# Prompt attention of a hybrid decoder layer on one core: query blocks outermost, several heads in one step for short blocks, half of the first output-projection tiles inside the last steps

## The reference, cut to what matters

```python
# q: 8 query heads of 64, in 2 kv groups (G) of 4 heads (R); 512 tokens
s = einsum('btgrd,blgd->btgrl', q, k_branch) * 64 ** -0.5
p = masked_softmax(s, k_pos <= q_pos)
o = einsum('btgrl,blgd->btgrd', p, v_branch)      # branch: selected, window
o_nsa = g0 * o_compressed + g1 * o_selected + g2 * o_window
# then
mix = concat([conv_y, o_nsa]) @ w_out             # 1024 -> 1024: the output projection
h = x + rms_norm(mix, g_post)
f = square(relu(rms_norm(h, g_pre2) @ w_up)) @ w_down
y = h + rms_norm(f, g_post2)
```

## Time and profile before

| what | value |
|---|---|
| runs of the kernel before | 785.29, 785.44, 789.34 us; median 785.44 us |
| the profiled execution | 784.3 us, its span 782.5 us |
| TensorE busy over the span | 749.1 us (96%) |
| VectorE, ScalarE, GpSimd busy | 472.0, 251.0, 316.0 us |
| chain that ended last, by engine | PE 86%, DVE 7%, ACT 3%, issue 2%, DMA 1% |
| prompt attention, 254.44 to 348.59 us | 94.15 us |
| one weight block, issue to landing | 4.8 us (median of 46) |
| loads of blocks 13 and 14 issued by the sync engine | from 250.83 us, 1.65 us for both |

### The profile page before, as it was taken

One profiled execution on the slowest core, in us unless ns is written; L12 is line 12 of the kernel. 1 busy time (PEld: TensorE's weight loads), 2 busy tenths in 40 slices (PEclk: granted clock), 3 DMA queues, 4 the chain that ended last, 5 costly groups with the idle time before them and its releaser, 6 DMA issues.

```text
span 782.5 us, 14992 instructions
## 1 busy us (share of the span) xinstructions
PE 749.1 (96%) x6243; PEld 696.1 (89%) x6243; DVE 472.0 (60%) x713; ACT 251.0 (32%) x457; POOL 316.0 (40%) x130
## 2 busy tenths in 40 slices
PE   8999999999998988989999999999999999999993
PEld 7999999987897555669999999999999999999993
DVE  5999978788767777752287334710025776732236
ACT  6412532233655677661443121300001112110021
POOL 1100000122301300002515577766865867876774
PEclk9999999999999999999999999999999999999997
DMA  9532421356625931001134121252122232133103
GB/s 357 186 109 89 149 84 34 118 182 219 222 90 163 254 60 54 2 1 54 55 109 161 55 107 60 102 214 92 69 107 80 84 107 103 59 108 107 54 1 109
DMA packets 25042, 85.51 MB, mean 109 GB/s; under 512 B 7216, under 2 KB 12896, under 8 KB 17760
## 3 DMA queue, kind: packets, MB, share of 16 engines
q1 hardware_dynamic: 17760, 62.13, 24.3%
q0 software_dynamic: 3456, 16.78, 6.3%
q10 hardware_dynamic: 3776, 5.89, 2.0%
HBM read 80.51 MB, written 8.47 MB: 114 GB/s over the span
## 4 chain that ended last, share of the span: by engine, by line
PE 86%; DVE 7%; ACT 3%; issue 2%; DMA 1%; SPq 0%; DVEq 0%; ACTq 0%
PE PA L1510 28%; PE PB L1510 28%; PE PB L1832 5%; DVE smx L1316 2%; PE PR L1930 2%; PE PR L1684 1%; PE PB L1521 1%; PE PA L1521 1%; PE PS L1705 1%; PE PB L1946 1%; DMA wraw<-wblk_dram 1%; PE PA L1669 1%; PE PR L1611 1%; PE PS L1954 1%; PE PS L1611 1%
## 5 line engine op out<-in xcount | busy, mean ns | idle before, releaser
L432 POOL TENSOR_TENSOR wH<-wraw,zero 128x2048 fp32r<-128x2048 f32 x29 | 105.3, 3631 | 110.6 <-PE PB L1510 87.1
L435 POOL TENSOR_TENSOR wL<-wraw,wH 128x2048 fp32r<-128x2048 f32 x29 | 139.5, 4811 | 2.3
L1412 DVE TENSOR_TENSOR hL<-h,hH 128x520 f32 (+1 forms) x32 | 64.6, 2022 | 47.1 <-ACT hH L876 47.1
L874 ACT ACTIVATE h<-rl 128x520 f32<-128x520 f32 x32 | 20.4, 638 | 209.3 <-DVE rl L1407 208.6
L992 DVE SCALAR_TENSOR_TENSOR yC<-uP,vec,yC 128x512 f32<-128x512 f32 (+1 forms) x135 | 84.3, 686 | 0.1
L1510 PE MATMUL PA<-hL,wH 128*128 128x260 f32 x240 | 67.7, 282 | 0.0
L1510 PE MATMUL PB<-hL,wH 128*128 128x260 f32 x240 | 67.7, 282 | 0.0
L1510 PE MATMUL PA<-hH,wL 128*128 128x260 f32 x240 | 67.7, 282 | 0.0
L1510 PE MATMUL PA<-hH,wH 128*128 128x260 f32 x240 | 67.7, 282 | 0.0
L1510 PE MATMUL PB<-hH,wH 128*128 128x260 f32 x240 | 67.7, 282 | 0.0
L1510 PE MATMUL PB<-hH,wL 128*128 128x260 f32 x240 | 67.7, 282 | 0.0
(11 more groups left out here) (517 smaller groups left out, 2311.1 us busy)
## 6 DMA issues: line engine op xcount, KB each, us to landing
wraw<-wblk_dram SPq DMA_DIRECT2D x46, 1024.0 KB, 4.8
xT<-x_fm_dram SPq DMA_DIRECT2D x4, 520.0 KB, 5.0
xT<-x_fm_dram SPq DMA_DIRECT2D x1, 2080.0 KB, 12.0
y_fm_dram<-xT SPq DMA_DIRECT2D x8, 260.0 KB
rkw<-cwk_dram SPq DMA_DIRECT2D x8, 256.0 KB, 2.7
s_win_dram<-cwk_dram ACTq DMA_DIRECT2D x1, 2044.0 KB
s_win_dram<-cwv_dram ACTq DMA_DIRECT2D x1, 2044.0 KB
p_rows_dram<-ktok ACTq DMA_DIRECT2D x4, 256.0 KB, 3.2
```

The source lines that it names most:

```text
L432: pool.tensor_tensor(wH[1 - s][:, :], wraw[s][:, :], zero[:, :].broadcast_to([P, BW]), ALU.add)\
L435: pool.tensor_tensor(wL[1 - s][:, :], wraw[s][:, :], wH[1 - s][:, :].bitcast(F32), ALU.subtract)\
L874: act.activation(h2[c % 2][:, :], rl[c % 2][:, :], ACT.Square).then_inc(s_h2, 1)
L1412: dve.tensor_tensor(lo, h2[c % 2][:, :], hi.bitcast(F32), ALU.subtract).then_inc(s_hl, 1)
```

## The change

The order of the prompt's attention is turned: the query block `i` is outermost, then the branch, then the heads. For block 0 (128 keys) all four heads, 128 keys each, form one step; for block 1 (256 keys) two heads form one step; for blocks 2 and 3 a step is one head as before. 32 steps become 22 (2, 4, 8 and 8). Every step now fills 1024, 768 or 1024 score columns over both groups. The exponentials, the scaling, masks, scores and transposes are issued for each head and group as before; maxima, sums, inverses, the copy of the transposes and the value products are issued once for all heads of the step. `PS[:, i % 2]` collects all four heads of one query block, `oH` and `oL` are written by query block, and the compressed branch enters by four matmuls of 128 columns for each block. The splits of weight blocks 13 and 14 move to steps 6 and 12 (ScalarE), 8 and 14 (VectorE), in the new count.

The first 260 columns of the output projection need query blocks 0 and 1, and the first four queries of block 2 (256 to 259). So the first half of tile 0 is issued inside the loop, in pass 23, between the transposes of step 20 and the values of step 19; the first half of tile 1 follows the loop, before the wait for the last block's split. The second halves come after it.

```diff
-PAIRS = [(r, br, i) for r in range(R) for br in range(2) for i in range(QT)]
-N_PAIRS = len(PAIRS)
-PER_R = 2 * QT
+HEADS = (((0, 1, 2, 3),), ((0, 1), (2, 3)), ((0,), (1,), (2,), (3,)), ((0,), (1,), (2,), (3,)))
+STEPS = [(rs, br, i) for i in range(QT) for br in range(2) for rs in HEADS[i]]
+N_STEPS = len(STEPS)
+PROBS = [sum(2 * len(rs) for rs, _, _ in STEPS[:n]) for n in range(N_STEPS + 1)]
+I_END = [sum(2 * len(HEADS[j]) for j in range(i + 1)) for i in range(QT)]
...
+            def out_hi(i):
+                act.wait_ge(s_pv, I_END[i])
+                act.activation(oH[:, :, i * P:(i + 1) * P], PS[:, i % 2, :].rearrange("p (r q) -> p r q", r=R),
+                               ACT.Copy).then_inc(s_oh, 1)
...
+                    act.activation(PTb[u % 2][:, :, 0:n], PR[:, :, 0:n], ACT.Copy).then_inc(s_ev, 1)
...
+                    for x in range(len(rs)):
+                        for g in range(G):
+                            c = PROBS[s] + g * len(rs) + x
+                            act.activation(Pb[s % 3][:, g, x * n:(x + 1) * n], PZ[s % 2][:, g, x * n:(x + 1) * n],
+                                           ACT.Exp, bias=smx[:, c:c + 1], accum_out=sms[:, c:c + 1]).then_inc(s_ex, 1)
...
-                if s in (8, 16):
-                    block_hi(13 if s == 8 else 14)
+                if s in (6, 12):
+                    block_hi(13 if s == 6 else 14)
+                for i in range(QT - 1):
+                    if s == I_END[i] + LAG + 2:
+                        out_hi(i)
+            out_hi(QT - 1)
...
+                    if len(rs) > 1:
+                        scores = PZ[s % 2][:, :, :].rearrange("p g (r n) -> p (g r) n", n=n)
+                    else:
+                        scores = PZ[s % 2][:, :, 0:n]
+                    dve.tensor_reduce(smx[:, PROBS[s]:PROBS[s + 1]], scores, AX.X, ALU.max, negate=True)\
+                        .then_inc(s_mx, 1)
...
+                    for x, r in enumerate(rs):
+                        for g in range(G):
+                            gc = 8 * (1 + br) + g * R + r
+                            c = PROBS[u] + g * len(rs) + x
+                            dve.tensor_scalar(Pb[u % 3][:, g, x * n:(x + 1) * n], Pb[u % 3][:, g, x * n:(x + 1) * n],
+                                              smr[:, c:c + 1], gtok[:, i, gc:gc + 1], ALU.mult, ALU.mult)\
+                                .then_inc(s_pn, 1)
...
-                if s in (10, 18):
-                    block_lo(13 if s == 10 else 14)
+                if s in (8, 14):
+                    block_lo(13 if s == 8 else 14)
...
+                    for g in range(G):
+                        for x in range(nr):
+                            for j in range(i + 1):
+                                mm = pe.transpose(PR[:, g, (j * nr + x) * P:(j * nr + x + 1) * P],
+                                                  Pb[u % 3][:, g, x * n + j * P:x * n + (j + 1) * P], ident[:, :])
                     mm.then_inc(s_T, 1)
...
+                if s == N_STEPS + 1:
+                    pe.wait_ge(s_cvl, CT)
+                    pe.wait_ge(s_ol, QT - 1)
+                    pe.wait_ge(s_split, SPLITS(B_OUT))
+                    pe.wait_ge(s_ex, PROBS[N_STEPS - 1])
+                    half_group(B_OUT % 2, 0, PA, actH, actL, 0)
...
+                    for x, r in enumerate(rs):
+                        for g in range(G):
+                            h = slice(g * HD, (g + 1) * HD)
+                            mm = pe.matmul(PZ[s % 2][:, g, x * n:(x + 1) * n], qT[h, r, i * P:(i + 1) * P],
+                                           kT[h, br, 0:n], start=False, stop=True, skip_group_check=True)
                     mm.then_inc(s_S, 1)
...
+                            mm = pe.matmul(PS[g * HD:(g + 1) * HD, i % 2, rs[0] * P:rs[0] * P + n],
+                                           vtok[:, br, j, g * HD:(g + 1) * HD], PTb[w % 2][:, g, j * n:(j + 1) * n],
                                            start=False, stop=(j == i), skip_group_check=True)
                     mm.then_inc(s_pv, 1)
...
-            pe.wait_ge(s_ol, R)
-            pe.wait_ge(s_ex, 2 * N_PAIRS)
-            for k in range(KT - 2):
+            pe.wait_ge(s_ex, PROBS[N_STEPS])
+            half_group(B_OUT % 2, 1, PB, actH, actL, 0)
+            pe.wait_ge(s_ol, QT)
+            half_group(B_OUT % 2, 0, PA, actH, actL, 1, s_grp)
+            half_group(B_OUT % 2, 1, PB, actH, actL, 1, s_grp)
+            for k in range(2, KT - 2):
```

More of the change, by code:

```diff
@@ L1326, in _ @@
                     dve.wait_ge(s_sm, 2 * u + 2)
[L1327 to L1332, removed]
+                    for x, r in enumerate(rs):
[5 more added lines that the diff above has]
+                                .then_inc(s_pn, 1)
+                if s == 4:
                     dve.wait_ge(s_dA, DA_OH)
@@ L1338, in _ @@
                                             oH[h, :, TP:T].bitcast(F32), ALU.subtract))
-                if s in (10, 18):
-                    block_lo(13 if s == 10 else 14)
[L1341 to L1348, removed]
+                if s in (8, 14):
+                    block_lo(13 if s == 8 else 14)
+                for i in range(QT - 1):
+                    if s == I_END[i] + LAG + 2:
+                        out_lo(i)
+            out_lo(QT - 1)
             dve.wait_ge(s_cst2, 32)
@@ L1513, in group, with half_group @@
                 mm.then_inc(s_grp, 1)
-            def half_group(s, c, pz, src_h, src_l, hf, done, k0=0, first=True):
+            def half_group(s, c, pz, src_h, src_l, hf, done=None, k0=0, first=True):
                 cols = slice(hf * HT, (hf + 1) * HT)
@@ L1902, in _ @@
             pe.wait_ge(s_initd, 2)
-            for s in range(N_PAIRS + LAG + 1):
+            for s in range(N_STEPS + LAG + 1):
                 u, w = s - LAG, s - LAG - 1
-                if s < N_PAIRS:
-                    r, br, i = PAIRS[s]
+                if s < N_STEPS:
+                    rs, br, i = STEPS[s]
+                    n = (i + 1) * P
                     if s >= 2:
-                        pe.wait_ge(s_ex, 2 * (s - 1))
+                        pe.wait_ge(s_ex, PROBS[s - 1])
                     for g in range(G):
-                        pe.matmul(PZ[s % 2][:, g, i * P:(i + 1) * P], identb[:, :], maskb[:, :], start=True, stop=False,
-                                  skip_group_check=True)
+                        for x in range(len(rs)):
+                            pe.matmul(PZ[s % 2][:, g, x * n + i * P:(x + 1) * n], identb[:, :], maskb[:, :],
+                                      start=(x == 0), stop=False, skip_group_check=True)
                 if s == 3:
@@ L1935, in _ @@
                         pe.wait_ge(s_dA, DA_OD)
-                    if r == 1:
+                    if i == 1:
                         pe.wait_ge(s_dV, DV_P + 4)
-                    if r >= 2:
-                        pe.wait_ge(s_ol, r - 1)
-                    pe.matmul(PS[:, r % 2, :], vcBD[:, r % 2, :], PcT[:, r // 2, :], start=True, stop=False,
-                              skip_group_check=True)
-                if s < N_PAIRS:
-                    r, br, i = PAIRS[s]
-                    for g in range(G):
-                        h = slice(g * HD, (g + 1) * HD)
-                        mm = pe.matmul(PZ[s % 2][:, g, 0:(i + 1) * P], qT[h, r, i * P:(i + 1) * P], kT[h, br, 0:(i + 1) * P],
-                                       start=False, stop=True, skip_group_check=True)
+                    if i >= 2:
+                        pe.wait_ge(s_ol, i - 1)
@@ new lines, in _ @@
+                    for r in range(R):
+                        pe.matmul(PS[:, i % 2, r * P:(r + 1) * P], vcBD[:, r % 2, :],
+                                  PcT[:, r // 2, i * P:(i + 1) * P], start=(r == 0), stop=False, skip_group_check=True)
+                if s < N_STEPS:
+                    rs, br, i = STEPS[s]
+                    n = (i + 1) * P
+                    for x, r in enumerate(rs):
[3 more added lines that the diff above has]
+                                           kT[h, br, 0:n], start=False, stop=True, skip_group_check=True)
```

70 lines of the change are left out of this document (31 added, 39 removed).

## The result

The changed kernel takes 777.92 us (median of 4 runs, 777.54 to 779.56), the kernel before on the same chip 786.32 us (median of 4, 785.29 to 789.34). The ratio is 0.9886 with a 95% interval of 0.9863 to 0.9909: 9.0 us or 1.1% faster, between 7.2 and 10.8. The forecast was 778.2 us. The profiled execution took 778.18 us with a span of 775.7, 6.8 us less than the 782.5 of before.

What follows compares the result with a forecast made beforehand. TensorE was taken to bound the prompt's attention, with 76.7 us of work in 94.15; 4.8 + 0.3 - 1.1 + 0 + 3.2 = 7.2 us less gave 778.2 us, with 773.5 to 782.0 as the range for 8 in 10.

Steps and rivals of the forecast that it cites:

- the stage: Prompt's attention: forecast from first scores to first projection matmul, 94.15 to 86.9 us; measured to the third projection tile.
- TensorE's work, 4.8 less: Attention steps of blocks 0 and 1: grouping heads cuts TensorE's work from 25.0 to 20.2 us.
- the ends: Score pairs in grouped steps: lower end nothing more (taken), upper end full lone-pair price, 2.0 us more.
- exposed loads: Rival on grouped score pairs: each pays a lone pair's price for its own weights, about 781 us; chance 0.13.
- The end, 3.2 less: From last scores to output projection: waiting falls from 4.2 to 1.0 us, half tiles alone worth 1.5.
- S+14.4: S is the end of step 21's scores; the half tile covering the last split ends 14.4 us later.
- The clock, 1.1 more: TensorE's half-clock loss in attention grows by 1.1 us, after a longer standstill before step 2's mask.
- the first dip: Clock drop in the filling, at 261 us: expected to grow from about 2 to 3 us.
- keep the second: Attention's second clock drop, at 312 to 315 us before: expected to stay, wherever it falls.
- a sign of being wrong: In the profile after, a clock dip over 5 us was listed as showing the forecast wrong.
- The filling and the rest, 0.3 less: Pipeline filling and short waits: 4.1 us of waiting plus 1.0 for block changes and `out_hi`, 5.1 for 5.4.
- The weight splits, 0: Splits of weight blocks 13 and 14 beside query blocks 2 and 3: TensorE's waits stay at 4.4 us.

Runs made afterwards that it cites:

- single_heads: Changed kernel with one head in every step (32 steps), query blocks outermost and half tiles moved; 785.0 us, ratio 0.9972 to the kernel before.
- order_only: Changed kernel with both halves of projection tiles 0 and 1 after the loop again, order and grouping kept; 781.1 us, ratio 0.9929 to the kernel before.
- keep_clock: Changed kernel with 44 and 22 idle matmuls before the masks of steps 2 and 3; 775.3 us, ratio 0.9854 to the kernel before.
- clock_and_sample: Changed kernel with sample_early's move plus 24 idle matmuls before step 3's mask and 8 before the first transposes; 776.2 us, ratio 0.9854.
- no_splits: Changed kernel with the splits of weight blocks 13 and 14 cut to one column each (stale weights); 773.0 us, ratio 0.9817.
- sample_early: Changed kernel with the sample group's 20 small matmuls in pass 2 before the mask's wait, not pass 3 after it; 775.4 us, ratio 0.9846.
- all_three: Changed kernel with the edits of clock_and_sample and quarters together; 770.8 us, ratio 0.9793 to the kernel before.
- quarters: Changed kernel with the splits of weight blocks 13 and 14 in quarters of 512 columns, one a step; 775.1 us, ratio 0.9846.

## Why the prediction was right, point by point

The forecast for the stage was 7.2 us less and 7.06 came. The terms were not all as good as their sum: the end brought 0.7 less than forecast and the clock cost 0.6 more, and the rest of the stage made up for both without having been forecast. That the sum came within 0.2 us is in part luck; that most of the gain is TensorE's work saved by the grouping is not.

- *TensorE's work, 4.8 less.* By the chain, a step of block 0 costs 0.45 + 0.88 + 1.12 + 1.01 = 3.46 us (forecast 3.51), one of block 1 0.33 + 0.88 + 1.06 + 1.01 = 3.28 (3.29), the compressed branch 0.89 for 0.86. That gives 25.0 - 20.0 - 0.1 = 4.9. single_heads, which takes back the grouping alone, loses 4.7, but with 1.7 us more of half clock in it and shorter waits in the filling (1.55 us, for 2.62 and 1.33), so that the two numbers are alike is no proof to the tenth. The choice between the ends was right: score pairs with weights of their own cost their columns and nearly nothing more. The forecast read the Trainium skill's rule on weight loads ("TensorE: Matmul & The Clock Gate", Part 3, The mechanism) as speaking for exposed loads, which would have shown as 1.3 to 1.7 us; in this trace they are not on the path. The reading was doubtful: by that rule a load overlaps matmuls of another row group, and the score products go to the two groups' 64 rows in turn, so that each load does have another row group than the product just before it.
- *The end, 3.2 less.* From the end of step 21's scores (332.67 us) to the second half of tile 0 (347.78) pass 15.11 us; without the two halves' usual 5.75 it is 9.36, with 7.7 of attention work and 1.7 of waiting, for 4.2 before: 2.5 less. (The forecast's 7.68 of work is 7.74 by its own rows.) The forecast put the end at S+14.4, it came at S+15.1. Its order of waits was right, that of step 20's transposes for the emptied `PR` included, but each came a little later: those transposes ended 0.3 us later than forecast, the last values 0.5 later, and the half tile that follows them took 3.08 us for 2.88. The part due to the half tiles was given as 1.5 us; order_only measures 1.8.
- *The clock, 1.1 more.* The step in it that failed is the size of the first dip, and with it "keep the second": there was one dip, not two, but of ten microseconds, twice the 5 us that the forecast itself had named as a sign of being wrong. By the windows it loses 3 x (0.31 + 0.50 + 0.50 + 0.40) = 5.1 us against 3.4 before, 1.7 more. That the longer standstill in the filling would cost clock was right in place and kind; keep_clock, which shortens it, and clock_and_sample, which removes it, speak for that.
- *The filling and the rest, 0.3 less.* The waits were forecast at 2.8 us before step 2's mask (2.62) and the first scaling's end at 263.9 (263.8). But the sample group's matmuls ran at half clock (4.6 us on the path for 2.5), so the values of step 1 ended at 279.7 us, where the forecast had 275.0 at full clock, or 278 with the 3 us of its dip. After that block 1 ran without a wait, as forecast (the forecast's 2.9 us for VectorE there is 3.0 with its own 1.22 for the maximum, still under TensorE's 3.3), and nothing was lost where the block size changes, where 1.0 us had been allowed. What is left once the other terms are taken off is 7.06 - 4.9 - 2.5 + 1.7 = 1.4 us less, for 0.3; this row was not measured by itself, so why it is larger stays open.
- *The weight splits, 0.* The waits are 0.94, 1.94, 1.01 and 0.51 us, 4.4 in all, as forecast, though not in the forecast's even pattern: VectorE's split of block 13 costs TensorE almost nothing, and the two of block 14, where the steps grow from 768 to 1024 columns, cost 3.5. no_splits prices them at 4.9.

The moved half tiles and splits made nothing later late: the third tile follows without a wait.

What stays open: the medians differ by more than the spans, 8.4 and 6.8 us. The profiled execution of before, 784.3 us, is under all of that kernel's other runs (784.5 to 790.5 us in two other sessions), so the spans may understate the gain. Its longer runs are those with the lower mean clock, 0.990 at 784.5 us and 0.981 at 790.2; where in the kernel their clock fell no profile shows. The forecast's own 7.2 lies at the edge of the measured 7.2 to 10.8.

## What to carry to other kernels

In a pipeline over several engines, grouping short steps into one pays by what it takes off the engine that sets the pace, and that can be added up from the chain of waits before building it; the maximum, the copy and the matmuls with shared columns then cost what their total size does. But the largest steps came to stand in the filling, where nothing hides them: put other work in the standstill, for the wait itself and for TensorE's clock after it. A side job that is longer than an engine's spare time in one step should be cut into pieces of that size, and work of the next stage that needs only early results can stand in the last steps, above all to cover the final split.

## What the runs showed of the hardware

- TensorE's clock falls to 1.2 GHz after standstills that are short: 2.62 and 1.33 us in the filling, or a single 1.94 us between dense steps (0.56 of full in 303 to 306 us of sample_early, 0.75 and 0.68 in clock_and_sample), but the same 1.94 us wait in the changed kernel, order_only and keep_clock was followed by windows at 1.00. With one profile of each, that can lie in the build or in the execution. The Trainium skill ("TensorE: Matmul & The Clock Gate", Why this matters for your kernels) warns that idle gaps between bursts bring the half clock; the traces agree that the clock falls behind gaps, though not behind every one.
- It can fall without a standstill: in keep_clock the gaps were filled up to 263.5 us, then came 20 matmuls of 8 and 64 columns, and the clock was 0.79 and 0.64 in the next windows. In clock_and_sample and all_three the same matmuls stood 6 us earlier in the stage and it stayed at 1.00. What tells the two apart was not tried.
- In four of the nine profiles of the changed kernel and its edits (single_heads, no_splits, quarters, clock_and_sample) the clock also fell in 249 to 255 us, ahead of everything that was edited, and the stage began 1.7 to 2.1 us later. Two windows of quarters:

```profile
249.00:252.00 3.00, 1.96 (x40) 1.91 (x41) 0.86 (x2) 0.79 (x2) 0.00 (x0) 0.69 0.70 262
252.00:255.00 3.00, 3.00 (x71) 2.78 (x64) 0.00 (x0) 0.00 (x0) 0.00 (x0) 0.74 0.64 213
```

The code there is the same in all nine, and so is the wait ahead of it (2.21 us, until 249.6 to 250.3 us), so the difference most likely lies in the execution and not in the edit. The runs' spans say the same: of six runs of quarters four have 773.1 to 773.3 us at a mean clock of 0.987 or 0.988, and two, the profiled one among them, 774.9 and 775.0 at 0.986 and 0.985; of five runs of sample_early two are 1.8 us shorter than the profiled one, at 0.990 for 0.987. So a dip that one profile shows, or lacks, may be different in the next run of the same kernel. Differences under 2 us between such kernels are read better from a stage of the trace than from medians, and of a single dip best from several profiles.
